# Memory attention of the samples: padded queries and probabilities stationary in 32-column tiles, keys and values moving

## The chip, the cores and the metric

The kernel runs on one core of one Trainium2 chip. The metric is the device time of one launch in microseconds, as the median of several runs. TensorE is PE in the profile (its weight loads PEld), VectorE is DVE, ScalarE is ACT, GpSimd is POOL; SyncE (SP) issues DMAs.

## The reference, cut to what matters

One inference step of a trunk of two layers, for a prompt (256 tokens) and 8 samples of 8 tokens (64), 320 tokens in all, model width 1024. Three branches work side by side in a layer: gated linear attention (GLA), retention, and attention over a memory of 256 rows with 4 heads of 128. The prompt's memory keys and values are computed; each sample brings its own (`cache_mem_k`, `cache_mem_v`). A ConvFFN with 2816 inner channels follows. Shortened:

```python
def memory_attention(q, mem_k, mem_v):
    s = jnp.einsum('blhd,bmhd->bhlm', q, mem_k).astype(jnp.float32) * (XA_DH ** -0.5)
    p = jax.nn.softmax(s, axis=-1).astype(mem_v.dtype)
    return jnp.einsum('bhlm,bmhd->blhd', p, mem_v)
...
    h = rms_norm(x, p['norm1_g'])
    proj = h @ p['w_in']
    gq, gk, gv, gr, ga, rq, rk, rv, rg, xq, gates = jnp.split(proj, split_at, axis=-1)
    log_a = jax.nn.log_sigmoid((ga @ p['gla_a_up'] + p['gla_a_b']).astype(jnp.float32)) / GLA_TAU
    o_gla, s_gla_new = chunked_gated_linear_attention(gq, gk, gv, log_a, s_gla, chunk)
    o_ret, s_ret_new = chunked_gated_linear_attention(rope(rq), rope(rk), rv, log_g, s_ret, chunk)
    o_xa = memory_attention(xq.reshape(B, L, XA_HEADS, XA_DH), mem_k, mem_v).reshape(B, L, -1)
    merged = (gate[:, :, 0] * (o_gla @ p['w_br_gla']) + gate[:, :, 1] * (o_ret @ p['w_br_ret'])
              + gate[:, :, 2] * (o_xa @ p['w_br_xa']))
    x = x + merged @ p['w_out']
```

For one sample, one head and all memory rows the scores are 8 x 256 and the output 8 x 128, each with a contraction of 128 or 256.

## The kernel before

All engines run programs written out by hand; semaphores join them, and the order of a program is the order of its engine. The activations stand with features on partitions and the 320 tokens on the free axis.

**Weights** come as a stream of 148 units a layer, 128 x 1024 f32 (512 KB) each. SP loads a unit into one of four slots `raw` (L224) once the copies of the unit before in that slot are made. ScalarE rounds it to `whi` (`hi`, L271), GpSimd makes the rest `wlo` in two steps (`lo`, L236, two slots), and PE takes three products for each weight tile: high by high, high by low, low by high. `unit` (L1067) is 24 matmuls with 320 moving columns, `vunit` (L1078) 18 with 512, `three` (L1036) serves branches, output and ConvFFN. ScalarE copies unit u + 4 after unit u is done, GpSimd's low part of unit u waits until u - 2 is done. Two banks A take the units in turn; ScalarE (or VectorE) empties them: `evac`.

**The stage around the change**, in PE's order: unit GA (the low-rank activation), XQ0 to XQ3 (memory queries), QK0 to QK7 (queries and keys of GLA and retention), GV0 to GV3 and RV0 to RV3 (values). Between the units stand the small f32 matmuls: prompt scores (L1177, 8 matmuls with 256 moving columns), transposes of probabilities (`turn`, L1132), probabilities by values (`pv`, L1138), the rotation of RoPE (`rot`, L1170), the low-rank product (L1183, `z_done`), and the samples' attention.

**Samples' attention.** `sample_scores` (L1148) makes, for one sample, one head and one half of the memory rows, a matmul with the keys stationary (128 x 128) and the 8 tokens of the queries moving; two samples a call, four calls a layer (behind QK4, QK5, QK6, QK7). The scores stand with memory rows on partitions in bank C[1]; ScalarE copies them (`sS`, L466), PE turns them in 4 transposes (L1211) so that tokens are on partitions, VectorE takes maxima (`xmaxes`, L727), ScalarE exponentials (`xexp_`, L380), VectorE the norm (`xnorm`, L735), PE turns the probabilities back (`turn(4)`), and `sample_values` (L1159) has values stationary and 8 probabilities moving, two samples a call, behind RV0 to RV3. ScalarE's `xhi(4)` and VectorE's `xlo(4)` split the result into high and low part. Caches have four slots; ScalarE issues the loads (`load_k`, `load_v`), two at a time.

**The low-rank chain.** The product of GA's result waits in PE's order until after QK1; then ScalarE adds the bias (L426), takes Abs (L429), Exp (L432) and Ln (L435), VectorE makes cumulative sums (L755, L757, L761, `b_ready`), ScalarE their exponentials (L442 to L444).

The prediction's other names: `outputs` (L1290, L1293, moving operands of 64 and 16 columns) and `chunk_updates` (L1249) belong to the gate stage that follows (`gated` units), `mem` parts to the stage ahead.

Of the kernel before, what the change touches and what calls it, by code (L numbers as in the profile page):

```python
# [23 lines left out]
P = 128  # L24
KT_ = D_MODEL // P
NS = DEC_BATCH * DEC_SEQ
T = SEQ + NS
# [20 lines left out]
def build_trunk(nc, w, x_in, mem_in, cache_k, cache_v, st_in, consts, final_g,  # L48
# [6 lines left out]
    with ctx:  # L55
# [55 lines left out]
        o_g = ar(24 * T)  # L111
# [8 lines left out]
        memK, memV, xq = at(o_g, 4, MEM), at(o_g + 1024, 2, 512), at(o_g + 2048, 4, T)  # L120
# [3 lines left out]
        sS = at(o_g + 9472, 512)  # L124
# [30 lines left out]
        hfp = [C[0], B[2], B[3]]  # L155
        UPB = ([C[0], C[1], A[0], A[1]], [B[2], B[3], C[0], C[1]])
# [23 lines left out]
        xk_used, xv_used, xst = sem("cache_k_used"), sem("cache_v_used"), sem("sample_scoresT_ready")  # L180
# [70 lines left out]
        def _(act):  # L251
# [62 lines left out]
            for lv in range(DEPTH):  # L314
# [77 lines left out]
                def xhi(e):  # L392
                    act.wait_ge(xo_done, lv * 5 + e + 1)
                    if e < 4:
                        i = nc.scalar.activation(oh[:, 8 + e, 0:SEQ], B[e][:, 0:SEQ], ACT.Copy)
                    else:
                        i = nc.scalar.activation(oh[:, 8:12, SEQ:T], C[1][:, 0:256].rearrange("p (h t) -> p h t", h=4), ACT.Copy)
                    i.then_inc(xoh, 1)

                def load_k(b):  # L400
                    act.wait_ge(xk_used, lv * 8 + b - 3)
# [22 lines left out]
                for p in range(2):  # L424
                    act.wait_ge(z_done, lv * 2 + p + 1)
                    link(nc.scalar.activation(zsb[:, p, :], C[p][:, 0:T], ACT.Identity, bias=par[:, C_AB + p:C_AB + p + 1]))  # L426
                wait_chain()
                for p in range(2):
                    link(nc.scalar.activation(ln1[:, p, :], zsb[:, p, :], ACT.Abs))  # L429
                wait_chain()  # L430
                for p in range(2):
                    link(nc.scalar.activation(bcum[:, p, :], ln1[:, p, :], ACT.Exp, scale=-1.0))  # L432
                wait_chain()
                for p in range(2):
                    nc.scalar.activation(ln1[:, p, :], bcum[:, p, :], ACT.Ln, bias=1.0).then_inc(ln_ready, 1)  # L435
                qk(2, qd[:, 0, :])
                qk(3, qd[:, 1, :])
                xturn(0)
                xturn(1)
                for p in range(2):  # L440
# [3 lines left out]
                    nc.scalar.activation(ee[:, p, :], ee[:, p, :], ACT.Exp, scale=1.0 / 16).then_inc(eb_ready, 1)  # L444
                xexp_(2)
                xexp_(3)
                qk(4, kd[:, 2, :])
                load_k(4)
                load_k(5)
# [5 lines left out]
                load_k(6)  # L455
                load_k(7)
                qk(6, qd[:, 2, :])
                load_v(0)
                load_v(1)
# [3 lines left out]
                load_v(2)  # L463
                load_v(3)
                act.wait_ge(xk_used, lv * 8 + 8)
                nc.scalar.activation(sS, C[1][:, :], ACT.Copy).then_inc(xst, 1)  # L466
                for u in (U_GV, U_GV + 1):
                    done(u)
                    hi(u + 4)
                xexp_(4)  # L470
                for u in (U_GV + 2, U_GV + 3):
# [5 lines left out]
                    if u == U_GV + 2:  # L477
                        xturn(4)
                for u in range(U_RV, U_SIL):
# [8 lines left out]
                    if u < U_RV + 2:  # L488
# [1028 lines left out]
```

## Time and profile before

| What | us |
|---|---|
| median of 3 runs | 1286.83 (1283.23 to 1287.61) |
| the profiled execution | 1282.97 |
| its span | 1281.2 |
| PE busy | 1247.3 (97%) |
| PEld busy | 1208.1 (94%) |
| POOL, DVE, ACT busy | 760.6, 642.2, 580.3 |
| mean granted TensorE clock | 0.976 |

The profile is of one execution. A busy PE is one with a matmul in its pipeline, not one at its peak; starts of matmuls are exact, ends are modelled, so the cost of a group is read from its first start to the next group's. The granted clock (PEclk) is a share of 2.4 GHz. Two layers do the same work, so most groups come twice.

### The profile page before, as it was taken

To read this page: it belongs to the slowest core of one execution; us is meant where nothing else is said; L and a number is where in the kernel's file an instruction comes from. 1 tells how busy PE (TensorE), PEld (TensorE's weight loads), DVE (VectorE), ACT (ScalarE), POOL (GpSimd) and SP (SyncE) were. 2 spreads that over 40 slices of the span, in tenths; PEclk is the share of its full clock that TensorE was granted. 3 is DMA by queue.
4 is the path that set the end of the run, shared out by engine and by line. 5 is a ranking of instruction groups with operands and counts; after the bars stand their busy time and mean duration, and the time that the engine had idled before them with its cause. 6 is when DMAs were issued, how large, how long until landed. Compare 5 with 4: busy or idle time off the path is not lost.

```text
span 1281.2 us, 23768 instructions
## 1 busy us (share of the span) xinstructions
PE 1247.3 (97%) x8240; PEld 1208.1 (94%) x8240; DVE 642.2 (50%) x1249; ACT 580.3 (45%) x948; POOL 760.6 (59%) x592
## 2 busy tenths in 40 slices
PE   5999999999999999999999999999999999999995
PEld 5899899999999999999989988999999999999995
DVE  5353327764685653155151431577647665504533
ACT  6472324434435664344456422344443466624442
POOL 4752435545577777777676333454547767777773
PEclk9998999999999999999999898999999999999998
DMA  7744434434454444454565433353434444444451
GB/s 271 243 145 155 138 112 152 123 120 138 150 151 144 149 147 148 148 149 149 157 236 170 150 131 131 118 156 129 134 116 148 148 138 151 151 151 148 147 154 58
DMA packets 53208, 190.73 MB, mean 149 GB/s; under 512 B 6032, under 2 KB 7312, under 8 KB 52880
## 3 DMA queue, kind: packets, MB, share of 16 engines
q1 hardware_dynamic: 43632, 159.15, 39.8%
q10 hardware_dynamic: 9504, 30.56, 6.5%
q8 instruction: 53, 0.87, 0.3%
q14 instruction: 19, 0.16, 0.0%
HBM read 181.15 MB, written 8.53 MB: 148 GB/s over the span
## 4 chain that ended last, share of the span: by engine, by line
PE 91%; DVE 3%; DMA 2%; ACT 1%; issue 1%; POOL 1%; SPq 0%; DVEq 0%; ACTq 0%; POOLq 0%
PE bank L1036 42%; PE bank L1067 29%; PE bank L1078 6%; PE bank L1148 2%; PE bank L1159 2%; DMA raw<-w 2%; PE bank L1272 1%; PE bank L1249 1%; PE bank L1293 1%; PE bank L1290 1%; PE bank L1138 1%; DVE arena L649 1%; POOL wlo L236 1%; DVE arena L912 1%; ACT whi L271 1%
## 5 line engine op out<-in xcount | busy, mean ns | idle before, releaser
L236 POOL TENSOR_TENSOR wlo<-raw,whi 128x512 fp32r<-128x512 f32 x588 | 760.4, 1314 | 501.7 <-PE bank L1067 261.3
L271 ACT ACTIVATE whi<-raw 128x1024 fp32r<-128x1024 f32 x294 | 310.7, 1057 | 293.2 <-PE bank L1036 165.8
L1067 PE MATMUL bank<-oh,whi 128*128 128x320 f32 x848 | 272.7, 322 | 3.4 <-DVE arena L930 2.1
L1067 PE MATMUL bank<-ol,whi 128*128 128x320 f32 x848 | 266.5, 314 | 0.0
L1067 PE MATMUL bank<-oh,wlo 128*128 128x320 f32 x848 | 266.3, 314 | 0.0
L1036 PE MATMUL bank<-hh,whi 128*128 128x320 f32 x832 | 257.8, 310 | 0.4 <-DVE hl L922 0.4
L1036 PE MATMUL bank<-hh,wlo 128*128 128x320 f32 x832 | 257.1, 309 | 0.0
L1036 PE MATMUL bank<-hl,whi 128*128 128x320 f32 x832 | 257.1, 309 | 0.0
L1067 PEld LDWEIGHTS bank<-oh,whi 128*128 128x128 f32 x848 | 163.6, 193 | 7.5 <-DVE arena L930 2.6
L1067 PEld LDWEIGHTS bank<-ol,whi 128*128 128x128 f32 x848 | 163.5, 193 | 0.6 <-issue 0.4
L1067 PEld LDWEIGHTS bank<-oh,wlo 128*128 128x128 f32 x848 | 163.2, 192 | 0.0
L1036 PEld LDWEIGHTS bank<-hh,whi 128*128 128x128 f32 x832 | 156.2, 188 | 1.1 <-DVE hl L922 0.9
L1036 PEld LDWEIGHTS bank<-hl,whi 128*128 128x128 f32 x832 | 156.2, 188 | 0.2
L1036 PEld LDWEIGHTS bank<-hh,wlo 128*128 128x128 f32 x832 | 156.2, 188 | 0.0
L1036 PE MATMUL bank<-oh,whi 128*128 128x320 f32 x416 | 128.5, 309 | 0.0
L1036 PE MATMUL bank<-ol,whi 128*128 128x320 f32 x416 | 128.5, 309 | 0.0
L1036 PE MATMUL bank<-oh,wlo 128*128 128x320 f32 x416 | 128.5, 309 | 0.0
L1036 PEld LDWEIGHTS bank<-oh,whi 128*128 128x128 f32 x416 | 78.1, 188 | 0.0
L1036 PEld LDWEIGHTS bank<-ol,whi 128*128 128x128 f32 x416 | 78.1, 188 | 0.0
L1036 PEld LDWEIGHTS bank<-oh,wlo 128*128 128x128 f32 x416 | 78.1, 188 | 0.0
L505 ACT ACTIVATE arena<-bank,par 128x320 f32<-128x320 f32 x48 | 25.3, 528 | 111.8 <-PE bank L1067 111.7
L998 DVE TENSOR_TENSOR x<-x,bank 128x320 f32<-128x320 f32 x32 | 13.5, 483 | 112.8 <-PE bank L1036 112.8
(191 smaller groups left out, 1639.9 us busy)
## 6 DMA issues: line engine op xcount, KB each, us to landing
raw<-w SPq DMA_DIRECT2D x296, 512.0 KB, 3.6
arena<-cache_k ACTq DMA_DIRECT2D x16, 512.0 KB, 6.0
arena<-cache_v ACTq DMA_DIRECT2D x16, 512.0 KB, 4.1
arena<-st_in ACTq DMA_DIRECT2D x8, 512.0 KB, 5.0
sst_out<-arena ACTq DMA_DIRECT2D x8, 512.0 KB, 3.3
con<-consts SPq DMA_DIRECT2D x1, 1288.0 KB, 13.1
x<-x_in SPq DMA_DIRECT2D x2, 640.0 KB, 10.2
arena<-mem_in SPq DMA_DIRECT2D x2, 512.0 KB, 6.3
```

Source lines behind the costliest of these rows:

```text
L236: i = pool.tensor_tensor(out=wlo[:, s % 2, h], in0=raw[:, s, h], in1=whi[:, s, h].bitcast(f32), op=ALU.subtract)
L271: nc.scalar.activation(whi[:, s, :], raw[:, s, :], ACT.Copy).then_inc(hi_ready, 1)
L505: nc.scalar.activation(G[:, j, :], A[u % 2][:, 0:T], ACT.Sigmoid, bias=par[:, C_BG + j:C_BG + j + 1]).then_inc(evac, 1)
L649: V.tensor_tensor(out=sqa[:, 0:width], in0=sqa[:, 0:width], in1=sq[(j - 1) % 2][:, 0:width], op=ALU.add).then_inc(sq_used, 2 if j == 1 else 1)
L912: link(V.reciprocal(gri[:, PART[j]], gri[:, PART[j]]))
L998: V.tensor_tensor(out=x[:, 4 * q + mm, :], in0=x[:, 4 * q + mm, :], in1=banks[q][mm][:, 0:T], op=ALU.add).then_inc(x_ready, 1)
L1036: r = MM(out, a, b, start=first and i == 0, stop=last and i == 2, skip_group_check=True)
L1067: r = MM(o, a, b[:, k, 0:n], start=k == 0 and i == 0, stop=k == KT_ - 1 and i == 2, skip_group_check=True)
L1078: r = MM(banks[a][:, :], x_[:, k, t0:t0 + P], w_, start=k == 0 and j == 0, stop=k == KT_ - 1 and j == 2, skip_group_check=True)
L1138: r = MM(B[e][:, 0:SEQ], memV[:, m, e * P:(e + 1) * P], pT[:, e % 2, m, :], start=m == 0, stop=m == 1, skip_group_check=True)
L1148: r = MM(C[1][:, o:o + 8], cache[:, b % 4, h * MEM + m * P:h * MEM + (m + 1) * P], xq[:, h, SEQ + 8 * b:SEQ + 8 * b + 8], start=True, stop ...
L1159: r = MM(C[1][:, o:o + 8], cache[:, b % 4, m * 512 + h * P:m * 512 + (h + 1) * P], pT[:, 0, m, b * 32 + h * 8:b * 32 + h * 8 + 8], start=m ...
```

## The change

The samples' queries and probabilities become the stationary operand, padded with zeros, and keys and values move. A stationary block has 32 columns: four samples by eight tokens, zero but for one sample's eight. The four samples of a group follow each other into the same 32 output rows and add up. The four heads go to four ranges of 32 output partitions. A call has four samples: two calls of scores (behind the prompt's scores, and behind `turn(3)`), two of values (behind GV2 and RV2). Scores now come out with tokens on partitions, so the copy `sS` and its 4 transposes go; the output comes out with tokens on partitions and is turned by 2 transposes (`oS`, `xot`). The zeroed area `padded` is cleared by VectorE in each layer; ScalarE writes queries (while it empties the bank) and probabilities (`pad_probs`) into it. The low-rank product moves up behind XQ0, its ScalarE steps between the evacuations of XQ1 to XQ3, its sums on VectorE ahead of the prompt's maxima; PE waits for `ln_ready` ahead of the first sample scores. Caches are loaded four at a time. The core of the diff:

```diff
@@ -117,11 +117,18 @@
         kTc = at(o_s + 4736, 2, NCH * DK)
         scm = at(o_s + 4096, 2 * T)
 
-        memK, memV, xq = at(o_g, 4, MEM), at(o_g + 1024, 2, 512), at(o_g + 2048, 4, T)
+        memK, memV, xq = at(o_g, 4, MEM), at(o_g + 1024, 2, 512), at(o_g + 2048, 4, SEQ)
         cache = at(o_g + 3328, 4, 1024)
         pp = at(o_g + 7424, 2, 2, MEM)
         pT = at(o_g + 8448, 2, 2, MEM)
-        sS = at(o_g + 9472, 512)
+        o_pad, PX = o_g + 9472, 544
+        padded = at(o_pad, PX + 512)
+
+        def pad(x, r, h):
+
+            return padded[:, x * PX + r * P + h * 32:x * PX + r * P + h * 32 + 32]
+
+        oS = pp[:, 1, 0, :]
 
         zsb, tmpa, ln1 = at(o_sil, 2, T), at(o_sil + 2 * T, 2, T), at(o_sil + 4 * T, 2, T)
         bcum, eb = at(o_sil + 6 * T, 2, T), at(o_gn, 2, T)
...
@@ -364,11 +379,28 @@
                 done(U_GA)
                 nc.scalar.activation(tmpa[:, 0, :], A[U_GA % 2][:, 0:T], ACT.Copy).then_inc(evac, 1)
                 hi(U_GA + 4)
+                act.wait_ge(pad_zero, lv + 1)
                 for h in range(4):
                     u = U_XQ + h
                     done(u)
-                    nc.scalar.activation(xq[:, h, :], A[u % 2][:, 0:T], ACT.Copy).then_inc(evac, 1)
+                    nc.scalar.activation(xq[:, h, :], A[u % 2][:, 0:SEQ], ACT.Copy)
+                    nc.scalar.activation(at(o_pad + h * 32, 2, 4, 136)[:, :, :, 0:8],
+                                         A[u % 2][:, SEQ:T].rearrange("p (a r t) -> p a r t", a=2, r=4), ACT.Copy).then_inc(evac, 1)
                     hi(u + 4)
+                    if h == 1:
+                        for p in range(2):
+                            act.wait_ge(z_done, lv * 2 + p + 1)
+                            link(nc.scalar.activation(zsb[:, p, :], C[p][:, 0:T], ACT.Identity, bias=par[:, C_AB + p:C_AB + p + 1]))
+                        wait_chain()
+                        for p in range(2):
+                            link(nc.scalar.activation(ln1[:, p, :], zsb[:, p, :], ACT.Abs))
+                    if h == 2:
+                        wait_chain()
+                        for p in range(2):
+                            link(nc.scalar.activation(bcum[:, p, :], ln1[:, p, :], ACT.Exp, scale=-1.0))
+                wait_chain()
+                for p in range(2):
+                    nc.scalar.activation(ln1[:, p, :], bcum[:, p, :], ACT.Ln, bias=1.0).then_inc(ln_ready, 1)
 
                 def xexp_(e):
 
...
-                    act.wait_ge(xo_done, lv * 5 + e + 1)
+                    if e < 4:
+                        act.wait_ge(xo_done, lv * 5 + e + 1)
+                    else:
+                        act.wait_ge(xot, lv + 1)
                     if e < 4:
                         i = nc.scalar.activation(oh[:, 8 + e, 0:SEQ], B[e][:, 0:SEQ], ACT.Copy)
                     else:
-                        i = nc.scalar.activation(oh[:, 8:12, SEQ:T], C[1][:, 0:256].rearrange("p (h t) -> p h t", h=4), ACT.Copy)
+                        i = nc.scalar.activation(by_four(oh[:, 8:12, SEQ:T]), sample_out, ACT.Copy)
                     i.then_inc(xoh, 1)
 
...
                     act.dma_start(cache[:, b % 4, :], cache_k[lv, b]).then_inc(cache_s[b % 4], 16)
 
                 def load_v(b):
-                    if b < 4:
-                        act.wait_ge(xk_used, lv * 8 + b + 5)
+                    if b < 3:
+                        act.wait_ge(xk_used, lv * 7 + b + 5)
+                    elif b == 3:
+                        act.wait_ge(xscore, lv * 5 + 5)
                     else:
                         act.wait_ge(xv_used, lv * 7 + b - 3)
...
-                    link(nc.scalar.activation(bcum[:, p, :], ln1[:, p, :], ACT.Exp, scale=-1.0))
-                wait_chain()
-                for p in range(2):
...
+                qk(3, qd[:, 1, :])
+                xturn(0)
+                xturn(1)
                 xexp_(2)
                 xexp_(3)
...
                 qk(4, kd[:, 2, :])
-                load_k(4)
-                load_k(5)
                 qk(5, kd[:, 3, :])
                 xhi(0)
                 xhi(1)
...
                 xturn(2)
...
                 xhi(3)
-                load_v(2)
-                load_v(3)
-                act.wait_ge(xk_used, lv * 8 + 8)
-                nc.scalar.activation(sS, C[1][:, :], ACT.Copy).then_inc(xst, 1)
-                for u in (U_GV, U_GV + 1):
-                    done(u)
-                    hi(u + 4)
-                xexp_(4)
-                for u in (U_GV + 2, U_GV + 3):
+
+                def pad_probs(a):
+
+                    act.wait_ge(xpt if a == 0 else xpt_ready, lv * 5 + 5)
+                    probs = C[1] if a == 0 else pT[:, 0].rearrange("p a b -> p (a b)")
+                    for m in range(2):
+                        i = nc.scalar.activation(at(o_pad + m * PX, 4, 136)[:, :, 0:P].rearrange("p r (h c) -> p r h c", c=32)[:, :, :, 0:8],
+                                                 probs[:, m * MEM + a * P:m * MEM + (a + 1) * P].rearrange("p (h r t) -> p r h t", h=4, r=4), ACT.Copy)
+                    i.then_inc(pad_ready, 1)
+
+                for u in range(U_GV, U_RV):
                     done(u)
                     if u == U_RV - 1:
                         for a in range(3):
                             nc.scalar.activation(vt[:, 0, a, :], B[a][:, :], ACT.Copy).then_inc(v_ready, 1)
                     hi(u + 4)
-                    if u == U_GV + 2:
+                    if u == U_GV + 1:
+                        pad_probs(0)
                         xturn(4)
+                for b in range(4, 8):
+                    load_v(b)
...
-                    if u < U_RV + 2:
-                        load_v(4 + 2 * (u - U_RV))
-                        load_v(5 + 2 * (u - U_RV))
+                    if u == U_RV + 2:
+                        act.wait_ge(xo_done, lv * 5 + 5)
...
                 dve.wait_ge(fg_s, 16)
+                if lv:
+                    dve.wait_ge(out_s["sst0"], lv * 32)
+                    dve.wait_ge(out_s["sst1"], lv * 32)
+                V.memset(padded, 0.0).then_inc(pad_zero, 1)
 
                 def xmaxes(e):
                     dve.wait_ge(xscore, lv * 5 + e + 1)
...
@@ -1122,6 +1156,10 @@
                 unit(U_GA, oh, ol, T, (hl_ready, lv * 16))
                 for h in range(4):
                     unit(U_XQ + h, oh, ol, T)
+                    if h == 0:
+                        pe.wait_ge(evac, lv * EVACS + 1)
+                        for p in range(2):
+                            MM(C[p][:, 0:T], par[:, C_AU + p * P:C_AU + (p + 1) * P], tmpa[:, 0, :], start=True, stop=True).then_inc(z_done, 1)
 
...
-
-                    for b in range(b0, b0 + 2):
-                        pe.wait_ge(cache_s[b % 4], lv * 64 + 16 * (1 + b // 4))
+                def sample_scores(a):
+
+                    for r in range(4):
+                        pe.wait_ge(cache_s[r], lv * 64 + 16 * (1 + a))
                         for h in range(4):
-                            for m in range(2):
-                                o = m * 256 + b * 32 + h * 8
-                                r = MM(C[1][:, o:o + 8], cache[:, b % 4, h * MEM + m * P:h * MEM + (m + 1) * P],
-                                       xq[:, h, SEQ + 8 * b:SEQ + 8 * b + 8], start=True, stop=True, skip_group_check=True)
-                        r.then_inc(xk_used, 1)
-
-                def sample_values(b0):
-
-                    for b in range(b0, b0 + 2):
-                        pe.wait_ge(cache_s[b % 4], lv * 64 + 16 * (3 + b // 4))
-                        for h in range(4):
-                            o = h * 64 + b * 8
-                            for m in range(2):
-                                r = MM(C[1][:, o:o + 8], cache[:, b % 4, m * 512 + h * P:m * 512 + (h + 1) * P],
-                                       pT[:, 0, m, b * 32 + h * 8:b * 32 + h * 8 + 8], start=m == 0, stop=m == 1, skip_group_check=True)
-                        r.then_inc(xo_done if b == 7 else xv_used, 1)
+                            i = MM(C[1][32 * h:32 * h + 32, a * MEM:(a + 1) * MEM], pad(a, r, h), cache[:, r, h * MEM:(h + 1) * MEM],
+                                   start=a == 0 and r == 0, stop=r == 3, skip_group_check=True)
+                        i.then_inc(xscore if a == 1 and r == 3 else xk_used, 1)
+
+                def sample_values(a):
+
+                    pe.wait_ge(pad_ready, lv * 2 + a + 1)
+                    for r in range(4):
+                        pe.wait_ge(cache_s[r], lv * 64 + 16 * (3 + a))
+                        for m in range(2):
+                            for h in range(4):
+                                i = MM(C[1][32 * h:32 * h + 32, a * P:(a + 1) * P], pad(m, r, h), cache[:, r, m * 512 + h * P:m * 512 + (h + 1) * P],
+                                       start=a == 0 and r == 0 and m == 0, stop=r == 3 and m == 1, skip_group_check=True)
+                        i.then_inc(xo_done if a == 1 and r == 3 else xv_used, 1)
 
...
 
+                pe.wait_ge(ln_ready, lv * 2 + 2)
+                sample_scores(0)
                 unit(U_QK + 1, oh, ol, T)
-                for p in range(2):
-                    MM(C[p][:, 0:T], par[:, C_AU + p * P:C_AU + (p + 1) * P], tmpa[:, 0, :], start=True, stop=True).then_inc(z_done, 1)
                 unit(U_QK + 2, oh, ol, T)
                 unit(U_QK + 3, oh, ol, T)
                 turn(0)
                 turn(1)
-                pe.wait_ge(ln_ready, lv * 2 + 2)
                 unit(U_QK + 4, oh, ol, T)
-                sample_scores(0)
                 unit(U_QK + 5, oh, ol, T)
-                sample_scores(2)
                 pv(0)
                 pv(1)
                 turn(2)
                 turn(3)
+                sample_scores(1)
                 unit(U_QK + 6, oh, ol, T)
-                sample_scores(4)
                 rot(0)
                 unit(U_QK + 7, oh, ol, T)
-                sample_scores(6)
                 pv(2)
                 pv(3)
                 rot(1)
                 toks = (0, P, T - P)
                 pe.wait_ge(xol, lv * 5 + 3)
                 vunit(U_GV, 0, oh, ol, toks, B)
-                pe.wait_ge(xst, lv + 1)
-                for a in range(2):
-                    for m in range(2):
-                        r = nc.tensor.transpose(C[1][:, a * MEM + m * P:a * MEM + (m + 1) * P], sS[:, m * 256 + a * P:m * 256 + (a + 1) * P], ident)
-                r.then_inc(xscore, 1)
+                turn(4)
                 vunit(U_GV + 1, 1, oh, ol, toks, B)
                 vunit(U_GV + 2, 2, oh, ol, toks, B)
+                pe.wait_ge(xpt_ready, lv * 5 + 5)
+                sample_values(0)
                 rot(2)
-                turn(4)
                 vunit(U_GV + 3, 3, oh, ol, toks, B)
                 rot(3)
-                pe.wait_ge(xpt_ready, lv * 5 + 5)
                 pe.wait_ge(evac, lv * EVACS + 13)
                 pe.wait_ge(xol, lv * 5 + 4)
 
@@ -1229,11 +1257,17 @@
 
                 for i in range(4):
                     vunit(U_RV + i, i, oh, ol, toks, RB)
-                    sample_values(2 * i)
+                    if i == 2:
+                        sample_values(1)
                     if i == 0:
                         pe.wait_ge(v_ready, lv * 6 + 3)
                         for p in range(3):
                             turn_keys(p)
+                pe.wait_ge(xos, lv + 1)
+                pe.wait_ge(rot_used, lv * 4 + 4)
+                for a in range(2):
+                    r = nc.tensor.transpose(C[0][:, a * P:(a + 1) * P], oS[:, a * P:(a + 1) * P], ident)
+                r.then_inc(xot, 1)
                 pe.wait_ge(kt_ready, lv * 4 + 3)
                 turn_keys(3)
 
```

## Rows read from the trace of the kernel before

**Rows 1.** The page: busy time of each engine, and the chain that ended last, by line

```profile
PE 1247.3 (97%) x8240; PEld 1208.1 (94%) x8240; DVE 642.2 (50%) x1249; ACT 580.3 (45%) x948; POOL 760.6 (59%) x592
...
PE bank L1036 42%; PE bank L1067 29%; PE bank L1078 6%; PE bank L1148 2%; PE bank L1159 2%; DMA raw<-w 2%; PE bank L1272 1%; PE bank L1249 1%; PE bank L1293 1%; PE bank L1290 1%; PE bank L1138 1%; DVE arena L649 1%; POOL wlo L236 1%; DVE ar
```

**Rows 2.** Groups by line and shape on PE and PEld: count, busy us, mean ns, idle before

```profile
L1148 PE MATMUL bank<-arena 128*128 128x8 f32 x256 | 31.0, 261 | 0.0
...
L1148 PEld LDWEIGHTS bank<-arena 128*128 128x128 f32 x256 | 31.4, 202 | 0.0
...
L1159 PE MATMUL bank<-arena 128*128 128x8 f32 x256 | 29.3, 254 | 0.0
```

**Rows 3.** Windows at sample groups (stretch; length; busy PE, PEld, DVE, ACT, POOL; PEclk; DMA)

```profile
88.37:91.86 3.49, 3.49 (x34) 3.49 (x33) 3.42 (x4) 2.49 (x8) 2.53 (x2) 1.00 0.50 173
...
105.16:109.81 4.65, 4.65 (x35) 4.65 (x33) 0.00 (x0) 1.38 (x2) 2.49 (x2) 0.74 0.46 159
...
719.01:723.15 4.14, 4.14 (x35) 4.14 (x33) 0.00 (x0) 1.38 (x2) 2.49 (x2) 0.84 0.01 4
```

**Rows 4.** Windows at the low clock: two around sample groups, one beside outputs

```profile
107.36:114.19 6.83, 6.83 (x27) 6.44 (x27) 2.48 (x6) 0.00 (x0) 0.60 (x1) 0.50 0.72 232
...
721.80:728.60 6.80, 6.80 (x25) 5.97 (x25) 0.85 (x2) 1.36 (x3) 0.00 (x0) 0.50 0.21 77
...
278.00:281.40 3.40, 3.40 (x15) 3.40 (x14) 3.24 (x10) 0.65 (x2) 0.00 (x0) 0.51 0.26 105
```

**Rows 5.** Windows of a unit at either clock, and of wider f32 groups

```profile
84.77:88.37 3.60, 3.60 (x27) 3.60 (x26) 3.53 (x4) 3.57 (x6) 2.35 (x2) 1.00 0.50 150
...
110.56:115.98 5.42, 5.42 (x26) 5.22 (x25) 2.48 (x6) 0.00 (x0) 0.00 (x0) 0.66 0.46 172
...
805.90:810.48 4.58, 4.58 (x41) 4.48 (x39) 2.92 (x9) 1.69 (x3) 2.51 (x2) 1.00 0.63 193
```

**Rows 6.** Timeline of PE: starts of the wider f32 groups and of what follows

```profile
68.89 3.61 PE L1177 MATMUL bank<-arena 128*128 128x256 f32 x16
...
72.16 0.50 PE L1067 MATMUL bank<-oh,whi 128*128 128x320 f32 x1
...
98.95 1.97 PE L1138 MATMUL bank<-arena 128*128 128x256 f32 x8
...
100.77 0.93 PE L1132 MATMUL bank<-con,arena 128*128 128x128 f32 x7
...
180.48 1.95 PE L1249 MATMUL bank<-arena 128*128 128x128 f32 x16
...
182.26 1.03 PE L1261 MATMUL bank<-qz,arena 128*128 128x256 f32 x4
```

**Rows 7.** Timeline of ACT and DVE along the low-rank chain, layer 0

```profile
76.39 1.05 ACT L271 ACTIVATE whi<-raw 128x1024 fp32r<-128x1024 f32 x1
...
77.34 0.94 ACT L426 ACTIVATE arena<-bank,par 128x320 f32<-128x320 f32 x2
...
80.02 1.28 ACT L435 ACT_TABLE_LOAD   x1
...
81.32 0.83 ACT L435 ACTIVATE arena<-arena 128x320 f32<-128x320 f32 x2
...
81.82 0.59 DVE L755 SCALAR_TENSOR_TENSOR arena<-arena 128x320 f32<-128x320 f32 x1 [6.07 <-ACT arena L435]
...
89.92 1.57 DVE L770 TENSOR_TENSOR arena<-arena 128x320 f32<-128x320 f32 x1
```

**Rows 8.** DVE by line in 60:180: the row maxima

```profile
L727 DVE TENSOR_REDUCE sml<-bank 128x2 f32<-128x512 f32 x5 | 3.4, 686 | 21.1 <-PE bank L1177 19.4 <-PE bank L1211 1.7
```

**Rows 9.** DMA issues of the page, and two windows with their rates

```profile
raw<-w SPq DMA_DIRECT2D x296, 512.0 KB, 3.6
...
714.90:718.30 3.40, 3.40 (x15) 3.40 (x14) 3.12 (x12) 1.47 (x4) 0.00 (x0) 0.51 0.88 317
...
61.70:181.00 119.30, 119.30 (x728) 110.50 (x727) 40.37 (x77) 47.74 (x88) 46.78 (x37) 0.93 0.44 145
```

More of the change, by code:

```diff
@@ L155, in build_trunk, with by_four @@
         hfp = [C[0], B[2], B[3]]
+        sample_out = C[0][:, 0:MEM].rearrange("p (a h s) -> p h a s", a=2, h=4)
+        def by_four(v):
+            return v.rearrange("p h (a s) -> p h a s", a=2)
         UPB = ([C[0], C[1], A[0], A[1]], [B[2], B[3], C[0], C[1]])
@@ L423, in _ @@
                 qk(1, kd[:, 1, :])
-                for p in range(2):
-                    act.wait_ge(z_done, lv * 2 + p + 1)
-                    link(nc.scalar.activation(zsb[:, p, :], C[p][:, 0:T], ACT.Identity, bias=par[:, C_AB + p:C_AB + p + 1]))
-                wait_chain()
-                for p in range(2):
-                    link(nc.scalar.activation(ln1[:, p, :], zsb[:, p, :], ACT.Abs))
-                wait_chain()
-                for p in range(2):
-                    link(nc.scalar.activation(bcum[:, p, :], ln1[:, p, :], ACT.Exp, scale=-1.0))
[L433 to L439, printed above, removed]
+                for b in range(4, 8):
+                    load_k(b)
                 for p in range(2):
@@ L454, in _ @@
                 xturn(3)
-                load_k(6)
-                load_k(7)
                 qk(6, qd[:, 2, :])
-                load_v(0)
-                load_v(1)
+                for b in range(4):
+                    load_v(b)
+                xexp_(4)
                 qk(7, qd[:, 3, :])
@@ L476, in _ @@
                     hi(u + 4)
-                    if u == U_GV + 2:
+                    if u == U_GV + 1:
+                        pad_probs(0)
                         xturn(4)
+                for b in range(4, 8):
+                    load_v(b)
+                pad_probs(1)
                 for u in range(U_RV, U_SIL):
@@ L745, in xlo @@
                     else:
-                        o, i0, i1 = ol[:, 8:12, SEQ:T], C[1][:, 0:256].rearrange("p (h t) -> p h t", h=4), oh[:, 8:12, SEQ:T]
+                        o, i0, i1 = (by_four(ol[:, 8:12, SEQ:T]), sample_out, by_four(oh[:, 8:12, SEQ:T]))
                     V.tensor_tensor(out=o, in0=i0, in1=i1.bitcast(f32), op=ALU.subtract).then_inc(xol, 1)
-                for e in range(4):
-                    xmaxes(e)
-                xnorm(0)
-                xnorm(1)
                 for p in range(2):
@@ L766, in _ @@
                             i.then_inc(b_ready, 1)
+                for e in range(4):
+                    xmaxes(e)
+                xnorm(0)
+                xnorm(1)
                 for p in range(2):
@@ L780, in _ @@
                 xlo(1)
+                xmaxes(4)
                 def rope(r):
@@ L803, in _ @@
                 rope(0)
+                xnorm(4)
                 xlo(2)
@@ L806, in _ @@
                 rope(1)
-                xmaxes(4)
-                xnorm(4)
                 rope(2)
```

10 lines of the change are left out of this document (6 added, 4 removed).

## The prediction

> **What bounds the kernel now.** I read the page first: PE, the TensorE matmul row, is busy 97% of a 1281.2 us span, and 86% of the chain that ended last is PE's lines of 1% and more [rows 1]. So I price PE's queue, and of the other engines only what PE would come to wait for. The chain gives most to the weight units (L1036, L1067, L1078); the two lines that the change rewrites, L1148 and L1159, have 2% each, about 56 us together.
>
> Then their rows by line and shape [rows 2]: 256 matmul records for each line, and as many weight loads. An f32 matmul leaves two pairs of load and matmul, so that is 128 matmuls a line, 64 a layer. Each has 128 stationary columns for 8 moving ones. The windows around the groups [rows 3] price them: one group (two batches, 16 matmuls, 32 records) takes 3.49 us at granted clock 1.00, or 0.109 us a record, with PEld busy throughout. There are 16 such windows in the kernel, two of them at a visibly lower clock. The one at 105.16 took 4.65 us at clock 0.74, the one at 719.01 4.14 at 0.84.
>
> That led me to the clock. Ten stretches in and right behind these groups run at 0.50, the lower of the two levels (1.2 GHz of 2.4), of which the two long ones are shown [rows 4]: in layer 0 one of 6.8 us and three of 3.4, in layer 1 one of 6.8 and five of 3.4, together 40.8 us. The clock falls after PE has run matmuls of 8 moving columns, and the price falls mostly on innocent neighbours: a unit of 24 matmuls takes 3.60 us at 1.00 and 5.42 at 0.66 [rows 5].
>
> **Term 1, the matmuls themselves.** Before: 8 groups a layer x 3.49 = 27.9 us at full clock. After: scores are two calls of 16 matmuls with 256 moving columns, values two calls of 32 with 128. What a record of such width costs: the 8 prompt score matmuls take 3.27 us (68.89 to 72.16) and the 4 of L1138 1.82 us (98.95 to 100.77), 5.09 us for 24 records, 0.212 each; the 128-column ones of L1249 take 1.78 us for 16 records, 0.111 each [rows 6]. Done one after another the new matmuls cost 64 x 0.212 + 128 x 0.111 = 13.6 + 14.2 = 27.8 us a layer: nothing is gained or lost. All depends on whether the four column tiles run side by side, and no row shows it, because every load of the trace is 128*128.
>
> The bounds. From above 27.8 us (one after another), plus a drain at every change of shape, below. From below 27.8 / 4 = 6.95 us, all four tiles at once. Between them I see two cases. If matmuls start in program order, the second record of an f32 matmul must wait for the first on the same tile, and only then can the next head's first record start beside it; then two tiles work at a time, and a layer costs 13.9 us. Or a record can't be issued more often than the 0.109 us of the narrow groups, where I can't tell issue from load; then it costs 64 x 0.109 + 128 x 0.109 = 21.0 us. I take 13.9: the order of the code (heads innermost, both records of a head together) points to it, and the price of 0.109 is met by 128-column loads, while the new loads have 32. Term: 2 layers x (27.9 - 13.9) = -28.0 us.
>
> The Trainium skill (TensorEngine Tiling, section Key Properties, and TensorE: Matmul & The Clock Gate, section Measured speedup) says that column tiles load and multiply independently, and has 2.38x for three column tiles and 3.07x for four row tiles, in another number format; by 3.07 a layer would cost 27.8 / 3.07 = 9.1 us and the time would be 10 us below my forecast. Its figures lie between my forecast and the first rival, which is the page's rule at its limit. The second page (section The mechanism) has a rule against this change: a weight load passes matmuls in flight only where the row groups differ, and here all four tiles use all rows. The trace does not agree for full-width tiles: in a unit PE and PEld are both busy for all of 3.60 us over the same rows, so loads pass matmuls in flight [rows 5]. No run here shows it for tiles; by that rule the time would be that of the third rival.
>
> **Term 2, the clock.** If the cause is the narrow moving operand, it goes. PE keeps 1.00 in stretches of 128- and 256-column f32 matmuls (805.90 to 810.48, 4.58 us) [rows 5]. 40.8 us at half speed would be 20.4 at full. I take -18.5, not all, since a slow stretch can come elsewhere too, as the one at 278.00, beside the 16-column matmuls that the change leaves alone [rows 4]. Bounds: 0 (stationary of 32 columns counts as little as moving of 8) and -20.4; the case below nothing is the fourth rival.
>
> **Term 3, switches and small pieces.** Eight entries and exits of the tiled shape a layer, 16 in the kernel. No row shows such a drain. It can be nothing beyond what the old groups' boundaries cost (they are in the 3.49 and 3.60 us), and at most one record left to finish, for which I take 0.31 us, above the 0.212 of rows 6 by half. I take 0.1 each, nearer to the boundaries shown: +1.6; bounds 0 and +5. Of the 4 score transposes a layer (0.1 each) 2 are left, on the output: -0.3 in all. The low-rank product keeps its 4 records.
>
> **Term 4, what PE may come to wait for.** PE now waits before the first sample scores for ScalarE's logarithm (ln_ready); behind that wait stands everything on PE. From the end of unit XQ1: two copies out of the bank 0.64 (an estimate by the 0.47 of one bias step), weight copy 1.05, bias 0.94, Abs 0.83 (as Ln); after XQ2 0.64 + 1.05 + table load 1.28 + Exp 0.83 (as Ln); after XQ3 the same with Ln [rows 7]. That is 3.5 + 3.8 + 3.8 = 11.1 us, and XQ3 ends at 7.0, so ln_ready comes about 4.2 us after XQ3. PE reaches its wait after one unit and the prompt scores, 3.5 + 3.3 = 6.8: hidden by 2.6 us. VectorE now does the cumulative sums ahead of the row maxima: 81.82 to 89.92 took 8.1 us for both halves [rows 7], until about 12; four maxima of 0.69 and a short scaling each, two norms that I put at 0.9 like them [rows 8]: the second probabilities are ready near 17.5. PE wants them at 6.8 + 3.4 + 3 x 3.5 = 20.7; with faster tiles at 19.0. Still hidden, by 1.5 to 3 us. ScalarE's qk(1) waits behind xexp_(1) until about 16 and frees bank A[1] for QK3 at 17.2: the tightest.
>
> The added ScalarE work (per layer 4 query copies, 4 padding copies, one output copy, less the 0.6 us copy of the scores) and the zeroing on VectorE (about 1 us) lie on engines busy 45% and 50% [rows 1], with their consumers one or more units later. The padding copies sit between the end of GV1 and the values, with GV2 (4.2 us) as cover for 1.05 + about 1.5.
>
> Cache loads go out four at once, not two. With one weight load beside them 5 x 0.524 MB at the 317 GB/s of the busiest window take 8.3 us, where a weight load alone lands in 3.6 [rows 9]. A slot is refilled when the low part is made, some 2.6 us after unit u ends, its copy on ScalarE stands two units later and the low part four: 4.4 us until ScalarE would wait, 10 until PE does. So a burst can hold ScalarE by about 4 us and PE by nothing or little. For all waits of this part: +2 us, bounds 0 and +10. Over the whole stage the supply is enough: 145 GB/s x 119.3 us [rows 9] in about 95 us is 182 GB/s.
>
> **Sum** against the profiled execution, 1283.0 us (span 1281.2): -28.0 - 18.5 + 1.6 - 0.3 + 2 = -43.2, so 1239.8. The median of the runs shown is 3.9 us above that execution, the lowest run equal to it; I put the median after at 1241.
>
> **Rivals.**
> First, all four tiles at once: 13.9 us less for both layers, some of it given back at the tightest wait above (+2): 1229. For it: tiles are four separate output ranges, with one signal a batch. Against: the two records of one tile stand together.
> Second, the floor per record of 0.109: 21.0 us a layer, 14.2 above the forecast: 1255. For it: no record in the trace comes faster than some 0.1. Against: none has a load under 128 columns.
> Third, the tiles don't run side by side, and the change does not do what it is for; only the clock is won: 1241 + 27.8 = 1269.
> Fourth, slower: the tiles run one after another, and an array with 32 of 128 columns in use lets the clock fall as the 8-column matmuls do. Each of the 8 calls, 6.9 us, runs half of itself and 3.4 us behind it at 0.50, as the groups of rows 3 and 4 do: 3.5 + 1.7 = 5.2 us a call, 42 in all, where 20.4 are paid now. 1269 + 18.5 + 21 = 1308. It decides from the point where both hold; with tiles side by side the calls are too short for it. For it: the clock has fallen only behind work that uses little of the array. Against: the one thing that all slow stretches follow is a moving operand of 8 or 16 columns, and the tiles' are 128 and 256.
> Fifth, the supply: a burst holds ScalarE's weight copies so long that PE waits, 1 to 2 us at each of 8 bursts: about 1253.
>
> **Chances.** Forecast 0.38, four at once 0.18, floor 0.12, one after another 0.18, slower with low clock 0.10, supply 0.04 (it can come on top of another). The range 1226 to 1272 takes all but the fourth rival and the tails of the others, about 0.2 left out. Within 0.3% (some 4 us, what a measurement can tell) the case of serial tiles with little of the clock won could fall: 0.04. Slower 0.10, faster 0.86.
>
> **What would show it.** The new score call of 32 records: 3.4 us by the forecast, 1.7 if four run, 3.5 by the floor (so the value call of 64 records decides: 3.5, 1.8 or 7.0), 6.8 and 7.1 if serial. Granted clock of 1.00 through and behind these calls, and no slow units beside them. PE with no idle time before the first score call and before QK3, ScalarE's weight copies with no more than 4 us on DMA after a burst. Wrong would be a PE row at 0.50 in the calls, calls of 6.8 us, or a wait on PE released by the padding copies.

## The result

| | before | after |
|---|---|---|
| median of the runs | 1285.03 us (4 runs, 1280.86 to 1287.61) | 1231.89 us (4 runs, 1231.62 to 1234.53) |
| profiled execution, span | 1282.97, 1281.2 us | 1232.07, 1230.3 us |
| mean granted clock | 0.976 | 0.991 |
| PE busy, PE records | 1247.3 us, 8240 | 1190.3 us, 8108 |

The ratio is 0.9588, interval 0.956 to 0.9617: 53 us less. The forecast was 1241, in a range of 1226 to 1272.

The page of the changed kernel, what answers to [rows 1]: the engines, and the chain by line.

```profile
PE 1190.3 (97%) x8108; PEld 1146.0 (93%) x8108; DVE 652.7 (53%) x1251; ACT 580.7 (47%) x964; POOL 764.5 (62%) x592
...
PE bank L1070 44%; PE bank L1101 28%; PE bank L1112 6%; DMA raw<-w 2%; PE bank L1306 1%; PE bank L1283 1%; PE bank L1327 1%; PE bank L1324 1%; DVE arena L679 1%; DVE arena L769 1%; POOL wlo L251 1%; DVE arena L946 1%; PE bank L1195 1%; PE bank L1184 1%; ACT whi L286 1%
```

PE is the bound as before, at the same 97%. The rewritten lines (now L1184 and L1195) have 1% each where they had 2%, and VectorE's L769, the norm of the probabilities, is new in the chain.

The two lines by form, against [rows 2] (count, busy us, mean ns, idle before):

```profile
L1195 PE MATMUL bank<-arena 128*32 128x128 f32 x256 | 7.8, 274 | 0.0
...
L1184 PE MATMUL bank<-arena 128*32 128x256 f32 x128 | 7.7, 382 | 0.0
```

Then windows: two score calls, two value calls, the turns with the products ahead of them, the stretch before GV0, a slow stretch, and layer 0's stage from GA to the f32 groups behind it. Columns as in [rows 3].

```profile
73.64:75.50 1.86, 1.86 (x34) 0.93 (x33) 1.75 (x5) 0.00 (x0) 0.00 (x0) 1.00 0.46 90
98.56:100.43 1.87, 1.87 (x34) 0.94 (x33) 0.03 (x1) 0.60 (x1) 0.00 (x0) 1.00 0.67 243
124.79:126.68 1.89, 1.89 (x66) 1.69 (x65) 0.00 (x0) 1.06 (x1) 1.67 (x2) 1.00 0.68 249
145.38:147.26 1.88, 1.88 (x65) 1.68 (x64) 0.00 (x0) 1.06 (x1) 1.67 (x2) 1.00 0.81 227
...
94.07:98.56 4.49, 3.13 (x18) 2.17 (x16) 4.35 (x9) 2.72 (x6) 2.54 (x2) 1.00 0.48 132
109.83:111.84 2.01, 0.71 (x4) 0.19 (x2) 1.96 (x4) 0.52 (x2) 1.08 (x1) 1.00 1.00 399
176.20:179.60 3.40, 3.40 (x15) 3.40 (x14) 3.22 (x10) 0.65 (x2) 0.00 (x0) 0.50 0.29 118
45.50:156.07 110.57, 106.79 (x750) 93.16 (x751) 49.15 (x88) 56.14 (x111) 57.88 (x44) 1.00 0.52 174
```

The first four are the answer to [rows 3]: 1.86 to 1.89 us a call where the forecast had 3.4 and 3.5, and 7.50 us a layer against 27.9. The last says that the whole stage of layer 0 now runs at clock 1.00; the ten slow stretches of [rows 4] are gone. Four are left outside, such as the one at 176.20 beside `outputs`; before there were three of that kind. It also says that PE is idle 3.8 us in the stage. 0.8 of them lie ahead of 61.7, where the kernel before idles as long; behind that it was never idle before [rows 9]. The new idle time has two places that matter, shown with their releasers (a third, of 0.3 us, stands at 152.48):

```profile
97.12 0.66 PE L1170 MATMUL bank<-con,arena 128*128 128x128 f32 x4 [1.17 <-DVE arena L769]
97.97 0.66 PE L1170 MATMUL bank<-con,arena 128*128 128x128 f32 x4 [0.19 <-DVE arena L769]
...
111.84 0.50 PE L1112 MATMUL bank<-whi,oh 128*128 128x512 f32 x1 [1.30 <-DVE ol L781]
```

**Where the 51 us of the profiled span came from.** A span times its mean granted clock is what it would be at full clock. Before: 1281.2 x 0.976 = 1250.5; after: 1230.3 x 0.991 = 1219.2. So 31.3 us are work and 19.6 clock, each known to about 1.3 us, as the clocks have three digits. The work: -2 x (27.9 - 7.5) = -40.8 for the matmuls; turns with the products ahead of them 4.49 us where it was 1.82 + 0.79, the rotation before GV0 2.01 where it was 0.30, the prompt scores 3.55 where it was 3.27: 3.9 us a layer, +7.7 in all; -0.3 for transposes. That is -33.4, some 2 us more than 31.3.

Run e3 (below) settles whether something is missing. It has the order of the kernel before, and its stages run at clock 1.00, so the stages can be compared as they are, from GA to the unit behind the f32 groups. First both layers of e3, then both of the changed kernel:

```profile
45.35:177.12 131.77, 130.87 (x855) 121.55 (x855) 47.77 (x96) 58.43 (x106) 59.18 (x46) 1.00 0.49 159
661.05:791.25 130.20, 129.65 (x855) 121.51 (x855) 43.16 (x86) 55.90 (x99) 59.03 (x46) 1.00 0.50 167
```

```profile
45.50:160.65 115.15, 111.37 (x788) 97.63 (x789) 51.58 (x96) 58.81 (x114) 60.39 (x46) 1.00 0.53 180
646.16:759.65 113.49, 110.13 (x789) 97.62 (x789) 46.44 (x85) 56.15 (x107) 60.44 (x46) 1.00 0.56 187
```

The stages are 16.6 and 16.7 us shorter, 33.3 in all. So the items above cover the stage, and the 2 us lie outside it or in the rounding of the clocks.

### The profile page after: what moved, and what is told of

The parts are those of the page before. It is cut to its first block, busy times and chain, and to the rows that moved or that the text cites. A ratio compares the mean times of both kernels' runs of the same rounds, so it can differ in the third digit from the quotient of the medians.

```text
span 1230.3 us, 23529 instructions
## 1 busy us (share of the span) xinstructions
PE 1190.3 (97%) x8108; PEld 1146.0 (93%) x8108; DVE 652.7 (53%) x1251; ACT 580.7 (47%) x964; POOL 764.5 (62%) x592
## 4 chain that ended last, share of the span: by engine, by line
PE 88%; DVE 6%; DMA 2%; issue 2%; ACT 1%; POOL 1%; SPq 0%; DVEq 0%; ACTq 0%; POOLq 0%
PE bank L1070 44%; PE bank L1101 28%; PE bank L1112 6%; DMA raw<-w 2%; PE bank L1306 1%; PE bank L1283 1%; PE bank L1327 1%; PE bank L1324 1%; DVE arena L679 1%; DVE arena L769 1%; POOL wlo L251 1%; DVE arena L946 1%; PE bank L1195 1%; PE bank L1184 1%; ACT whi L286 1%
## 5 line engine op out<-in xcount | busy, mean ns | idle before, releaser
L251 POOL TENSOR_TENSOR wlo<-raw,whi 128x512 fp32r<-128x512 f32 x588 | 764.3, 1321 | 446.9 <-PE bank L1101 233.9
```

Source lines behind the costliest of these rows:

```text
L251: i = pool.tensor_tensor(out=wlo[:, s % 2, h], in0=raw[:, s, h], in1=whi[:, s, h].bitcast(f32), op=ALU.subtract)
```

## The experiments

A column tile is one of the four ranges of 32 output partitions, one for each head. The diffs are shortened to what they do.

**e1, one head at a time.** The changed kernel, only the order of the tiled matmuls turned (scores shown, values alike):

```diff
-                    for r in range(4):
-                        for h in range(4):
+                    for h in range(4):
+                        for r in range(4):
                             i = MM(C[1][32 * h:32 * h + 32, a * MEM:(a + 1) * MEM], pad(a, r, h), ...)
```

> The changed kernel with only the order of the tiled matmuls turned: all matmuls of one head, so of one column tile, then the next head's. The same matmuls, the same output. Theory (four tiles run side by side only where neighbours in PE's order go to different tiles): a score call takes 6.8 us in place of 1.87, a value call 7.1 in place of 1.88, so 8 calls cost 41 us more, 1232 + 41 = 1273. Rival (each tile has a queue of its own, so order does not matter): calls stay at 1.9 us, 1232. On the clock: if a stationary operand of 32 columns counted as little as a moving one of 8, one tile at a time would let it fall to 0.50 in and behind these calls, and the time would be near 1300; if the moving operand decides, it stays at 1.00.

Measured 1259.47 us (1257.6 and 1261.35), 27.6 more than the changed kernel. Windows of a score call and two value calls:

```profile
73.22:77.75 4.53, 4.53 (x34) 2.39 (x33) 4.29 (x12) 1.40 (x7) 0.00 (x0) 1.00 0.37 119
129.70:135.59 5.89, 5.89 (x66) 5.69 (x65) 0.00 (x0) 1.06 (x1) 2.51 (x2) 1.00 0.54 171
154.29:160.17 5.88, 5.88 (x65) 5.68 (x64) 0.00 (x0) 1.06 (x1) 2.51 (x2) 1.00 0.61 178
```

Order decides, but both theories had the size wrong: 4.5 and 5.9 us, not 6.8 and 7.1, and not 1.9. PE's timeline inside the first call says why. Eight records of head 0 are due, 0.216 us apart; the row that begins at 74.11, after only four starts, has eight starts in the next 0.9 us:

```profile
73.22 1.05 PE L1186 MATMUL bank<-arena 128*32 128x256 f32 x4
...
74.11 1.06 PE L1186 MATMUL bank<-arena 128*32 128x256 f32 x8
```

Head 1 starts while head 0 has some four records unfinished. It looks as if a column tile takes about that many ahead and the engine then moves on to the next tile's; that is a theory of its own, tested in e8. The clock stays at 1.00 with one tile or two at work, in the calls and from 73.22 to 168.99 as a whole, so the fourth rival of the prediction is dead: 32 stationary columns don't let it fall here.

**e2, two heads at a time**: heads 0 and 1 through all four samples, then 2 and 3.

```diff
-                    for r in range(4):
-                        for h in range(4):
+                    for g in (0, 2):
+                        for r in range(4):
+                            for h in (g, g + 1):
```

> The changed kernel with the heads in two pairs: only two column tiles take turns at a time. Theory (side by side with the neighbours in order): two tiles at a time, calls of 3.4 to 3.6 us, 8 x 1.6 = +13 us, 1245. Rival (own queues): 1.9 us a call, 1232. This is also the value of 13.9 us a layer that the prediction took for all four tiles.

Measured 1242.91 us (1240.71 and 1245.1), 11 more. Calls, scores then values:

```profile
73.91:76.66 2.75, 2.75 (x34) 1.42 (x33) 2.61 (x7) 0.00 (x0) 0.00 (x0) 1.00 0.54 185
126.86:130.08 3.22, 3.22 (x65) 3.02 (x64) 0.00 (x0) 1.06 (x1) 2.51 (x2) 1.00 0.39 156
```

Two tiles work at a time: for the scores 2 x 8 x 0.216 = 3.5 us, less 0.7 of overlap where the pairs change. So order decides here too, with calls shorter than the expected 3.4 to 3.6. The time is near the 1241 that I had forecast for the change itself, but not by the same sum: these calls cost 11.9 us a layer and not 13.9, and the waits cost more than I had put.

**e8, two matmuls of a head together**: runs of four records on one tile (values: the two halves of the memory rows; scores: two samples).

```diff
-                        for m in range(2):
-                            for h in range(4):
+                        for h in range(4):
+                            for m in range(2):
```

> The changed kernel with two f32 matmuls of one head (four records on one column tile) ahead of the next head's two. In e1_one_head_at_a_time the next head's first record starts while some four records of the head before are still to run. Theory (a tile takes about four records ahead, and the engine goes on to the next tile's): runs of four fit, all four tiles work at once in the middle of a call, calls of 1.9 to 2.3 us, 1232 to 1235. Rival (a tile holds one record beside the running one, and the next tile starts only behind that): each run of four holds the others up for two, calls of about 3.5 us, 1245.

Measured 1234.36 us (1233.46 and 1235.26); calls of 1.90 us for scores, 1.95 and 1.96 for values, a few hundredths over the changed kernel. So runs of four records lose nothing to speak of, longer ones do (e1 puts eight or sixteen on one tile, e2 as many on each of two tiles, before the next). The theory of e1 holds; the rival, 3.5 us, is out. The limit is each tile's own and not one for all: in e8 the fourth head starts 0.04 us behind the first, past nine records that wait on three tiles, and in e1 the next head is held up by fewer than that on a single tile.

**e3, wider moving operands in the kernel before.** Nothing else changed; the samples' attention is computed from other numbers.

```diff
-                                r = MM(C[1][:, o:o + 8], cache[...], xq[:, h, SEQ + 8 * b:SEQ + 8 * b + 8], ...)
+                                r = MM(C[1][:, o:o + 96], cache[...], xq[:, h, T - 96:T], ...)
```

> The kernel before, with nothing changed but the width of the moving operand of the samples' matmuls: 96 columns in place of 8 (the columns beside the sample's own are computed and written too, so the samples' attention comes out of other numbers; the count of instructions and the order stay). 96 columns in two passes are 80 ns a record, under the 109 ns that the 128-column load takes, so the groups should stay at 3.49 us. Theory (the clock fell for the narrow moving operand): none of the ten stretches at 0.50 in the two attention stages, and 20 us less, 1265. Rival (it falls for something else there, such as the many weight loads or f32): stretches stay, 1285.

Measured 1267.72 us (1267.11 and 1268.33), ratio 0.9847 (0.9737 to 0.9958). Two groups and the stage:

```profile
88.38:91.87 3.49, 3.49 (x34) 3.49 (x33) 3.39 (x5) 2.46 (x8) 2.58 (x2) 1.00 0.56 161
...
165.15:168.69 3.54, 3.54 (x33) 3.54 (x32) 0.00 (x0) 2.51 (x4) 2.50 (x2) 1.00 0.00 0
61.70:173.00 111.30, 111.30 (x728) 103.53 (x727) 40.35 (x77) 47.47 (x88) 46.71 (x37) 1.00 0.47 151
```

The groups cost what they did before (3.49 to 3.54 us) with twelve times the columns, and the stage runs at 1.00 where [rows 9] has 0.93. Span times clock is 1265.3 x 0.989 = 1251.4, the kernel before's 1250.5 again within the rounding. So the clock term is shown by itself: the gain, 17 us against the median of 1285.03 and 22 against the 1289.89 of the kernel before beside it, came from the width of the moving operand, not from tiles or from fewer instructions.

**e4, the same with 32 columns.**

> As e3_moving_96, with 32 moving columns in place of 8 (27 ns of streaming in a record of 109). Theory (the share of a record in which the array streams decides): at 32 columns the clock falls as often as at 8, or nearly: 5 to 10 stretches at 0.50 in the two attention stages, 1275 to 1287. Rival (any width over the sample's own 8 will do): none, 1266.

Measured 1274.9 us (1274.34 and 1275.46). The stretches at the score groups are gone, where the kernel before had five. At the value groups there are six at the lower level (1.2 GHz), three a layer, where it had five; two of them here.

```profile
61.70:144.90 83.20, 83.20 (x539) 77.62 (x538) 36.72 (x68) 39.30 (x75) 39.07 (x30) 1.00 0.44 146
144.90:148.30 3.40, 3.40 (x15) 3.11 (x15) 1.76 (x6) 1.48 (x3) 0.00 (x0) 0.50 0.56 165
155.10:158.50 3.40, 3.40 (x11) 2.72 (x11) 0.00 (x0) 0.00 (x0) 0.00 (x0) 0.50 0.87 280
```

Six lies in the expected 5 to 10, and the time 0.1 us below its range. Neither theory said that scores and values would part; why they do is open.

**e5, the low-rank product moved up alone**, in the kernel before: PE's two products behind XQ0, ScalarE's and VectorE's steps with them, as in the diff of the change.

> The kernel before with the second part of the change alone: the low-rank product behind XQ0, ScalarE's steps of it between the evacuations of XQ1 to XQ3, VectorE's sums ahead of the row maxima. Theory (the new PE waits of 3.3 us a layer in the changed kernel come from the lost cover of the long sample groups, not from this order): no PE wait at the turns and before GV0, 1285 within 3. Rival (they come from the order of VectorE): PE waits of 1 to 3 us a layer here too, about 1290.

Measured 1286.67 us (8 runs, 1279.24 to 1296.93), ratio 0.9984 (0.9938 to 1.0031): no difference. PE has no wait at the turns or before GV0. So the second part of the change neither brings nor costs time by itself, and the new waits need the short sample calls. Whether short calls would bring them in the old order as well was not run. What the second part does is free bank C[1] for the early scores.

**e6, keys early.** VectorE multiplies the decays into the keys as soon as QK1 is out of its bank, and only the queries wait for QK3.

```diff
                 for p in range(2):
                     dve.wait_ge(eb_ready, lv * 2 + p + 1)
-                    dve.wait_ge(evac, lv * EVACS + 9)
+                    dve.wait_ge(evac, lv * EVACS + 7)
...
+                dve.wait_ge(evac, lv * EVACS + 9)
+                for p in range(2):
                     V.scalar_tensor_tensor(out=qd[:, p, :], ...).then_inc(qd_ready, 1)
```

> The changed kernel with one wait of VectorE split: the decayed keys (ke, kd) wait for the evacuation of QK1 (7 of evac) in place of QK3 (9), and only the decayed queries (qd) wait for QK3. In the changed kernel VectorE stands idle 4.3 us before them (82.6 to 86.9) and then hands the second pair of probabilities over late, for which PE waits at the turns 1.2 + 0.2 us, with 1.9 us lost there by the starts. Theory (VectorE's order is what is late): the wait at the turns goes, 1.5 to 1.9 us a layer, 3 to 4 in all, 1228. Rival (ScalarE's exponentials, or GpSimd slowing VectorE down, are what is late): the wait stays, 1232.

**e7, keys early and low parts first**: as e6, and

```diff
                 rope(0)
-                xnorm(4)
                 xlo(2)
                 xlo(3)
+                xnorm(4)
                 rope(1)
```

> As the one before, and VectorE takes the low parts of heads 2 and 3 ahead of the norm of the samples' probabilities. Before GV0 PE waits 1.3 us (1.7 by the starts) for the low part of head 2, which stands behind that norm. Theory: this wait falls to about 0.3, another 1 to 1.5 us a layer, 1225.5. Rival (the rotation's steps in front are late anyway): no more than 0.5 us a layer, 1227 to 1228.

**after_again**, the changed kernel beside them on the same chip:

> The changed kernel again, on the same chip as the next two, as their yardstick: 1232 within 2, granted clock 0.991.

Measured: the changed kernel 1232.40 us (1231.66 to 1234.78), e6 1230.84 (1227.57 to 1233.74), e7 1226.32 (1225.22 to 1228.03), five runs each; against the kernel before e7 is 0.9522 (0.9503 to 0.954). VectorE in the changed kernel, ahead of the late probabilities:

```profile
80.99 1.59 DVE L769 TENSOR_SCALAR arena<-arena,sml 128x256 f32<-128x256 f32 x2
86.90 1.20 DVE L804 TENSOR_TENSOR arena<-arena 128x320 f32<-128x320 f32 x1 [4.32 <-ACT arena L451]
```

and in e7, with windows of its turns and of the rotation before GV0:

```profile
82.72 0.49 DVE L804 TENSOR_TENSOR arena<-arena 128x320 f32<-128x320 f32 x1
```

```profile
94.29:96.99 2.70, 2.70 (x19) 2.28 (x17) 2.48 (x4) 2.38 (x5) 2.39 (x2) 1.00 0.58 194
108.26:108.90 0.64, 0.64 (x3) 0.19 (x1) 0.45 (x2) 0.51 (x2) 0.64 (x1) 1.00 0.99 378
```

The 4.32 us of idle VectorE go, the turns with their products take 2.70 us in place of 4.49, and the rotation 0.64 in place of 2.01. In e6 PE has no wait left at the turns, but the 1.30 us before GV0 stay. e6's times overlap the changed kernel's because the clock scatters (0.986 to 0.992 over its runs); by span times clock it is 1214.7 to 1216.0 against 1218.3 to 1219.4, some 3.6 us, in the expected 3 to 4, though the median is not the expected 1228. e7 is 1211.5 to 1213.1 by the same measure, some 6.5 us, so the second wait was worth 1.5 us a layer and its theory holds too. e7 is 6 us faster than the changed kernel, and the two ranges lie apart.

The order is not all that made the probabilities late. VectorE and GpSimd in the changed kernel, at the norm of heads 2 and 3:

```profile
94.50 2.57 DVE L769 TENSOR_SCALAR arena<-arena,sml 128x256 f32<-128x256 f32 x2
97.18 0.74 DVE L769 TENSOR_SCALAR arena<-arena,sml 128x256 f32<-128x256 f32 x2
```

```profile
94.38 2.54 POOL L251 TENSOR_TENSOR wlo<-raw,whi 128x512 fp32r<-128x512 f32 x2 [0.75 <-PE bank L1101]
```

The same pair of instructions takes 0.74 us alone and 2.57 beside GpSimd's low part. Over both layers the eight of L769 that run alone take 0.35 us each, and ten of the twelve that overlap L251 take 1.2 to 1.4. The 1.8 us lost here are more than the 1.17 + 0.19 that PE waits. e6 shows that an earlier start is enough to hide it; what a free GpSimd would give was not run.

## Why the prediction was right, and where it was wrong

The time lies in the range, and the sign and the place were right. The mechanism of the main term was not the forecast's but that of the first rival, all four tiles at once (1229), to which I gave 0.18. That the time is within 9 us of 1241 is in part luck, as the sum below shows.

**Term 1 failed in one step**, the one that chose 13.9 us a layer: "the second record of an f32 matmul must wait for the first on the same tile, and only then can the next head's first record start beside it". The first half is true (records of a tile start 0.216 or 0.109 us apart), the second is not. Waiting records stand at their own tile, some three behind the running one, and the next head's start meanwhile (e1, e8). So -28.0 should have been -40.8. The price of a record by width (0.212, 0.111), the serial total of 27.8 and the lower bound of 6.95 (measured 7.50) held; the floor of 0.109 us a record was false, as a value call has 64 records in 1.88 us, 0.029 each.

The Trainium skill (TensorE: Matmul & The Clock Gate, section Measured speedup vs the span model) has 2.38x for three column tiles; its table names no number format. Here four tiles give 27.8 / 7.5 = 3.7x over the serial price, so the trace goes further.

The rule that spoke against the change is that of the Trainium skill (TensorE: Matmul & The Clock Gate, section The mechanism): loads pass matmuls in flight only where row groups differ. The trace does not agree. PEld starts 32 tile loads within the 1.86 us of a score call, over the same rows as the 32 matmuls beside them.

**Term 2 held**: -18.5 forecast, -19.6 by span times clock, and e3 shows the cause alone.

**Term 3 held in size**: +1.6 was put for entries and exits of the tiled shape. 7.50 less 6.95 is 0.55 us a layer inside the calls. As much lies ahead of them: the prompt scores take 3.55 us in place of 3.27 before the first call, and ahead of each of the other three the first record comes 0.09 us later than the spacing before it. That is some 2.2 us in all.

**Term 4 was mis-sized**: +2 forecast, +7.0 measured (the 7.7 of the result less 0.7 for the entries). The wait that I checked first (ln_ready) stayed hidden with about the margin forecast: ScalarE's last Ln ends at 70.36 and PE wants it at 73.64, 3.3 us later, where I had 2.6. The tightest one (QK3) did not come either, nor did the bursts of cache loads cost PE anything that the trace shows. The two that came I had not priced: the second pair of probabilities, late because VectorE stands in order behind a wait for QK3 and is slowed beside GpSimd, and the low part of head 2 behind the samples' norm. Before the change four sample groups of 3.49 us stood between and hid both; e5 shows that they did. The rule "say what is late next" was applied to what the change moved, not to what its long groups had covered.

Terms 1 and 4 erred in opposite directions: 12.8 us too little gain and 5.0 too little cost. With the small errors of the others, and the 2 us that are not placed, the profiled execution came out 7.7 us under the sum of 1239.8, and the median 9 under 1241.

## What to carry to other kernels

Small f32 matmuls with a narrow output can go to four column tiles at nearly a quarter of the serial price, if no more than about four records in a row go to one tile (measured with 128 and 256 moving columns). When long groups of PE work become short, list every wait that they covered, along each in-order queue, before counting the gain. A group of matmuls with a few moving columns costs more than its own time: look at the granted clock of the neighbours behind it.

## What the runs showed of the hardware that was not expected

The scatter of the kernel before is its clock. Over nine runs on one chip its times went from 1280.48 to 1294.98 us with clocks from 0.978 to 0.967, while span times clock stayed between 1250.3 and 1252.0. The changed kernel scatters by 3 us. So the change also took away most of the noise, and span times granted clock tells apart kernels 3 us from each other where medians don't (e6), as far as three digits of clock allow, some 0.6 us.

Column tiles keep a few records each, and it is a count and not a time. In e1 head 1's first record starts right behind the fifth of head 0's eight in a score call (74.117 and 74.111) and right behind the thirteenth of its sixteen in a value call (131.041 and 131.035). Three records are left behind the one that just started both times, though the records are 0.216 us apart in the one and 0.109 in the other.
